# A transformer stack on one core: sparse attention worked in pairs of heads, products of ones placed in three waits of PE, and score maxima taken per query tile

## The chip, the core and the metric

The kernel is written in Bass, instruction by instruction, for one NeuronCore of a Trainium2 chip. The engines are PE (TensorE), DVE (VectorE), ACT (ScalarE), POOL (GpSimd) and SP, which issues most DMAs. Each runs its own list of instructions in order and waits on semaphores. The metric is the device time of one execution in microseconds (us), as the median of the runs shown.

## What is computed

Two blocks run one after the other on 256 tokens of 1,024 features, all in float32. The first has a state-space mixer with stick-breaking attention, cross attention to a memory, and a squared-ReLU feed-forward layer. The second has a gated convolution (its products are called pw1 and pw2 below), a convolutional feed-forward layer, the sparse attention that is changed here, and another feed-forward layer. The sparse attention of 16 heads of 64 features sums three branches, each with its own softmax and gate:

```python
return gt[..., 0:1] * o_c + gt[..., 1:2] * o_s + gt[..., 2:3] * o_w
```

`o_c` attends to 15 compressed keys. `o_s` (selected blocks) and `o_w` (window) see, at this length of 256 tokens, every key up to the query, with different keys and values: 4 groups of keys, each shared by 4 heads. So a branch of a head is a causal softmax over 256 keys: the first 128 queries see 128 keys, the second 128 queries see 256, together 384 columns of scores in 128 partitions.

## The kernel before

**Products of weights.** Weights stream from memory in chunks of 128x1024 numbers (`WR`). ACT rounds a chunk to the high part (`WH`, line 1254), DVE subtracts to get the low part (`WL`, line 1504), three chunks ahead of PE. `tile` multiplies a chunk with eight pieces (k = 0 to 7) of the activations, themselves in a high and a low part (`XH`, `XL` or `YH`, `YL`), three matmuls for each k (lines 876 to 878). Where the activations come just in time, the first tile waits for each k (`base=`), and with `norm=` it also sums the squares for the norm (`sum_square`, line 884, the product with `ONES`). `RS`, the factor of that norm, is only known when the tile has ended; DVE waits for it at the start of the program before it splits chunk 2.

**The first instructions.** PE waits for `ones_done`, then its first tile waits for chunk 0's low part and k = 0 of `XL`. DVE makes `XL` for k = 0 to 3, then `WL` of chunk 0 (`sp.to(1)`), then `XL` for the rest.

**Preparation of the sparse attention.** Twelve chunks of keys and queries pass through a per-head norm and a rotation. For the four chunks of keys, DVE adds the two terms of the rotation in two instructions of 64 partitions (line 638) into `KZ`, where the keys of the one head of a pair stand in partitions 0 to 63 and those of the other in 64 to 127, and the other half is zero.

**The attention.** One step is one head `hh`, both branches. Names: `big` holds the scores (2 of its 4 banks for a head), `mis` the turned weights, `acc` the outputs. The engines run these loops, each in the order written:

- PE: `scores` (two products and one of the mask for each branch, the queries as weights, all 128 rows), `turn` of the head before (6 transposes into `mis`), `outputs` of the head before that (6 products), and after each second head `pair`, which adds the compressed branch (line 493, 32 rows) and turns both heads' summed outputs (line 496).
- DVE: maxima of the scores (one instruction of 768 columns, line 781, which gives six numbers), a minimum of two of them (784), reciprocals of the sums (791), a copy of the second branch out of `mis` (795), the factors with the gates (798), the outputs times the factors (807), their sum (820), the low part `YL` (814).
- ACT: a copy of the first branch out of `mis` (586), four exponentials with their sums (593), the high part `YH` (605).
- POOL does nothing in it.

`scores` of a head waits for the exponentials two heads before (two buffers). The products of the output weights (`nsa_out`) follow.

## Time and profile before

| | |
|---|---|
| three runs | 1142.57, 1143.38, 1145.54 us; median 1143.38 |
| the profiled execution | 1141.42 us, span 1139.6 us |
| granted TensorE clock, mean | 0.988 of full |
| PE / DVE / ACT / POOL busy | 94% / 69% / 47% / 11% of the span |
| chain that ended last | PE 77%, DVE 13%, ACT 5%, issue 3%, POOL 1%, DMA 1% |

The span runs from the first to the last instruction of the profiled execution. A view over time gives for each row the start, the time to the end of the last one merged in it, engine, line and operation, the tile written and those read, the shape, and how many follow each other; in brackets the idle time before it and what ended it. The ends of matmuls are modelled and overlap the next, so the distance from one start to the next is what a matmul takes of PE. A float32 matmul stands as two instructions, one with the rounded types as one. A window gives its length, then for PE, PE's weight loads, DVE, ACT and POOL the busy time (and the instructions), the granted TensorE clock, the busy share of DMA, and GB/s. `64*128` stands for the rows and columns of the array that a matmul uses.

### The profile page before, as it was taken

To read this page: it belongs to the slowest core of one execution; us is meant where nothing else is said; L and a number is where in the kernel's file an instruction comes from. 1 tells how busy PE (TensorE), PEld (TensorE's weight loads), DVE (VectorE), ACT (ScalarE), POOL (GpSimd) and SP (SyncE) were. 2 spreads that over 40 slices of the span, in tenths; PEclk is the share of its full clock that TensorE was granted. 3 is DMA by queue.
4 is the path that set the end of the run, shared out by engine and by line. 5 is a ranking of instruction groups with operands and counts; after the bars stand their busy time and mean duration, and the time that the engine had idled before them with its cause. 6 is when DMAs were issued, how large, how long until landed. Compare 5 with 4: busy or idle time off the path is not lost.

```text
span 1139.6 us, 22909 instructions
## 1 busy us (share of the span) xinstructions
PE 1076.3 (94%) x8721; PEld 1023.1 (90%) x8721; DVE 788.4 (69%) x1314; ACT 534.6 (47%) x917; POOL 122.7 (11%) x140
## 2 busy tenths in 40 slices
PE   5999889799999989997999999997989999999998
PEld 4999679699999989877999999996878999999998
DVE  4876667655567767685776776759866667777676
ACT  5453555544443453217644444455435545444442
POOL 0060020011123300002001001040110000100100
PEclk9999999899999999999999999999999999999999
DMA  8563205255554634221565555663530025655551
GB/s 316 153 195 99 94 21 184 76 177 183 183 175 158 205 117 149 75 76 57 165 204 184 175 192 186 179 166 117 186 111 1 2 75 172 198 176 192 181 184 61
DMA packets 46438, 165.25 MB, mean 145 GB/s; under 512 B 5153, under 2 KB 6177, under 8 KB 46241
## 3 DMA queue, kind: packets, MB, share of 16 engines
q1 hardware_dynamic: 45216, 163.24, 45.1%
q10 hardware_dynamic: 1152, 1.05, 0.4%
q8 instruction: 49, 0.80, 0.3%
q14 instruction: 21, 0.16, 0.0%
HBM read 162.17 MB, written 1.05 MB: 143 GB/s over the span
## 4 chain that ended last, share of the span: by engine, by line
PE 77%; DVE 13%; ACT 5%; issue 3%; POOL 1%; DMA 1%; DVEq 0%; SPq 0%; ACTq 0%
PE acc L876 15%; PE acc L878 14%; PE acc L877 14%; PE big L876 6%; PE big L878 6%; PE big L877 6%; DVE WL L1504 4%; PE mis L884 2%; DVE CD L1871 2%; PE acc L480 2%; ACT WH L1254 2%; PE big L451 1%; PE acc L937 1%; PE acc L938 1%; PE acc L939 1%
## 5 line engine op out<-in xcount | busy, mean ns | idle before, releaser
L1504 DVE TENSOR_TENSOR WL<-WR,WH 128x1024 fp32r<-128x1024 f32 x302 | 378.8, 1269 | 148.4 <-ACT WH L1254 139.2
L876 PE MATMUL acc<-XH,WH 128*128 128x256 f32 x1392 | 404.8, 291 | 20.7 <-DVE WL L1504 13.2
L878 PE MATMUL acc<-XH,WL 128*128 128x256 f32 x1392 | 395.4, 284 | 0.0
L877 PE MATMUL acc<-XL,WH 128*128 128x256 f32 x1392 | 395.1, 284 | 0.0
L1254 ACT ACTIVATE WH<-WR 128x1024 fp32r<-128x1024 f32 x302 | 312.2, 1051 | 126.0 <-PE acc L878 82.7
L876 PEld LDWEIGHTS acc<-XH,WH 128*128 128x128 f32 x1392 | 268.2, 193 | 25.3 <-issue 17.8
L877 PEld LDWEIGHTS acc<-XL,WH 128*128 128x128 f32 x1392 | 267.8, 192 | 1.3
L878 PEld LDWEIGHTS acc<-XH,WL 128*128 128x128 f32 x1392 | 267.8, 192 | 0.0
L876 PE MATMUL big<-UH,WH 128*128 128x256 f32 x608 | 170.9, 281 | 0.9 <-POOL UL L1990 0.8
L877 PE MATMUL big<-UL,WH 128*128 128x256 f32 x608 | 169.6, 279 | 0.0
L878 PE MATMUL big<-UH,WL 128*128 128x256 f32 x608 | 169.6, 279 | 0.0
L1990 POOL TENSOR_TENSOR UL<-GU,UH 128x256 fp32r<-128x256 f32 x76 | 56.3, 741 | 679.0 <-ACT UH L1394 679.0
L876 PEld LDWEIGHTS big<-UH,WH 128*128 128x128 f32 x608 | 114.4, 188 | 1.9 <-POOL UL L1990 1.1
L878 PEld LDWEIGHTS big<-UH,WL 128*128 128x128 f32 x608 | 114.2, 188 | 0.0
L877 PEld LDWEIGHTS big<-UL,WH 128*128 128x128 f32 x608 | 114.1, 188 | 0.0
L1394 ACT ACTIVATE UH<-GU 128x256 fp32r<-128x256 f32 x76 | 31.8, 418 | 168.8 <-DVE GU L1782 95.6
L876 PE MATMUL acc<-YH,WH 128*128 128x256 f32 x256 | 75.9, 296 | 7.6 <-POOL YL L1986 6.5
L877 PE MATMUL acc<-YL,WH 128*128 128x256 f32 x256 | 73.2, 286 | 0.0
L878 PE MATMUL acc<-YH,WL 128*128 128x256 f32 x256 | 73.2, 286 | 0.0
L876 PEld LDWEIGHTS acc<-YH,WH 128*128 128x128 f32 x256 | 49.9, 195 | 10.7 <-issue 6.3
L877 PEld LDWEIGHTS acc<-YL,WH 128*128 128x128 f32 x256 | 50.1, 196 | 0.1
L878 PEld LDWEIGHTS acc<-YH,WL 128*128 128x128 f32 x256 | 49.9, 195 | 0.0
(296 smaller groups left out, 1294.7 us busy)
## 6 DMA issues: line engine op xcount, KB each, us to landing
WR<-weights SPq DMA_DIRECT2D x302, 512.0 KB, 3.6
X<-x_t SPq DMA_DIRECT2D x4, 256.0 KB, 6.2
MEM<-mem_t SPq DMA_DIRECT2D x1, 1024.0 KB, 9.7
result_t<-X SPq DMA_DIRECT2D x4, 256.0 KB, 2.2
CON<-constants SPq DMA_DIRECT2D x1, 896.0 KB, 11.8
CBUF<-KCV ACTq DMA_DIRECT2D x4, 128.0 KB, 5.4
CBUF<-KCV ACTq DMA_DIRECT2D x4, 127.5 KB, 6.5
SML<-small_weights SPq DMA_DIRECT2D x1, 480.0 KB, 14.2
```

What stands on the lines that cost most here:

```text
L451: pe.matmul(o[:, P:P + T], QP[:, j, P:T], k, start=False, stop=True, skip_group_check=True)
L480: ins = pe.matmul(acc[:, 0, (2 * br + tt) * P:(2 * br + tt) * P + P], PT[:, hh % 2, br, b * P:b * P + P], NV[:, m, 128 * g + 64 * br:128 * ...
L876: pe.matmul(out, wh, hi, start=start, stop=False, skip_group_check=True)
L877: pe.matmul(out, wh, lo, start=False, stop=False, skip_group_check=True)
L878: return pe.matmul(out, wl, hi, start=False, stop=stop, skip_group_check=True)
L884: ins = pe.matmul(mis[:, 0, 0:T], ONES[:, :], SQ[:, k], start=k == 0, stop=k == n - 1, skip_group_check=True)
L937: pe.matmul(o, xh, wh, start=kk == 0, stop=False, skip_group_check=True)
L1254: act.activation(WH[:, cs % SPL], WR[:, cs % RAW], ACT.Copy).then_inc(w_high, 1)
L1394: act.activation(UH[:, us % 2], GU[:, us % 2], ACT.Copy).then_inc(u_high, 1)
L1504: dve.tensor_tensor(WL[:, cs % SPL], WR[:, cs % RAW], WH[:, cs % SPL].bitcast(F32), ALU.subtract).then_inc(w_low, 1)
L1871: ins = dve.scalar_tensor_tensor(o, x, w, o, ALU.mult, ALU.add)
L1990: pool.tensor_tensor(UL[:, us % 2], GU[:, us % 2], UH[:, us % 2].bitcast(F32), ALU.subtract).then_inc(sem("u_low"), 1)
```

## The change

A step of the attention is now one branch of a pair of heads, still 16 steps. The scores of the two heads come from the two halves of the array's rows (64 features each, so `KR` needs no zeros), their outputs go through the two halves of its columns, and sum over branches in `acc` with the compressed branch, feature by feature, so the turn of the outputs is gone. The weights are normalised and gated before they are turned, by POOL, in three instructions. There are three buffers of weights instead of two, and `turn` and `outputs` run three and four steps behind `scores`. The second query tile's scores stand first in a bank, so that DVE takes the maxima in two instructions, one for each query tile, and the minimum is gone. `idle_passes` multiplies `ONES` with itself, 25 times at the start, 11 times before pw1 and 18 times before pw2; nothing reads the results. DVE makes `WL` of chunk 0 ahead of `XL`. PE waits for the seventh `YL` before `nsa_out`.

```diff
@@ -171,15 +171,15 @@
+                   ("QN", [P, 8, T], F32), ("QP", [P, 8, T], F32), ("KN", [P, 2, T], F32), ("KR", [P, 4, T], F32),
...
+        def PP(i):
+
+            flat = (CBUF.rearrange("p a g t -> p (a g t)")[:, 0:768], CBUF.rearrange("p a g t -> p (a g t)")[:, 768:1536],
+                    HS.rearrange("p a b t -> p (a b t)")[:, 1536:2304])[i % 3]
+            return flat.rearrange("p (e n) -> p e n", e=2)
+
+        PT = HS.rearrange("p a b t -> p (a b t)")[:, 0:1536].rearrange("p (s e n) -> p s e n", s=2, e=2)
@@ -439,63 +442,53 @@
+            pe.wait_ge(sem("kr_done"), 4)
...
+            def scores(i):
+                j, br = i // 2, i % 2
+                k = KR[:, 2 * br + j // 4, :]
+                if i >= 2:
+                    pe.wait_ge(sem("at_exp"), i - 1)
+                for q, o, n in ((slice(P, T), 0, T), (slice(0, P), T, P)):
+                    for e in range(2):
+                        h = slice(64 * e, 64 * e + 64)
+                        pe.matmul(big[:, 2 * br + e, o:o + n], QP[h, j, q], k[h, 0:n], start=o == 0, stop=True,
+                                  skip_group_check=True)
+                for e in range(2):
+                    ins = pe.matmul(big[:, 2 * br + e, P:P + T].rearrange("p (c n) -> p c n", c=2), IDR[:, :], NCR[:, :, :],
+                                    start=False, stop=True, skip_group_check=True)
                 ins.then_inc(sem("at_s"), 1)
 
+            def turn(i):
+                pe.wait_ge(sem("at_pn"), i + 1)
+                if i >= 1:
+                    pe.wait_ge(sem("at_pt"), i)
+                for e in range(2):
                     for b in range(3):
-                        ins = pe.transpose(mis[:, br, b * P:b * P + P], PP[:, hh % 2, br, b * P:b * P + P], con("ident"))
+                        c = (b + 1) % 3
+                        ins = pe.transpose(mis[:, e, c * P:c * P + P], PP(i)[:, e, b * P:b * P + P], con("ident"))
                 ins.then_inc(sem("at_t"), 1)
 
+            def outputs(i):
+                j, br = i // 2, i % 2
+                o = acc[:, j % 2, 0:T]
+                if br == 0:
+                    q = slice(32 * (j % 4), 32 * (j % 4) + 32)
+                    if j == 0:
+                        pe.wait_ge(sem("pct_done"), 1)
+                    if j >= 2:
+                        pe.wait_ge(yl_ready, Y_BASE["nsa"] + j - 1)
+                    pe.matmul(o, VB[q, j // 4, :], PCT[q, j // 4, :], start=True, stop=False, skip_group_check=True)
+                pe.wait_ge(sem("at_pt"), i + 1)
+                for m in range(2):
+                    for e in range(2):
+                        v = 128 * (2 * (j // 4) + e) + 64 * br
+                        ins = pe.matmul(o[64 * e:64 * e + 64, m * P:T], NV[:, m, v:v + 64],
+                                        PT[:, i % 2, e, m * T:m * P + T], start=False, stop=br == 1 and m == 1,
+                                        skip_group_check=True)
                 ins.then_inc(sem("at_o"), 1)
...
+            for i in range(STEPS + 4):
+                if i < STEPS:
                     scores(i)
-                if i == 1:
                     turn_compressed()
+                if 3 <= i <= STEPS + 2:
+                    turn(i - 3)
+                if i >= 4:
+                    outputs(i - 4)
@@ -578,37 +569,33 @@
+            for i in range(STEPS + 5):
+                if i < STEPS:
+                    act.wait_ge(sem("at_nm"), 2 * i + 2)
                     if i >= 3:
+                        act.wait_ge(sem("at_t"), i - 2)
+                    for e in range(2):
+                        for tt, (a, b) in ((1, (0, T)), (0, (T, P + T))):
+                            ins = act.activation(PP(i)[:, e, a:b], big[:, 2 * (i % 2) + e, a:b], ACT.Exp,
+                                                 bias=RM3[:, i % 3, e, 2 - 2 * tt:3 - 2 * tt],
+                                                 accum_out=RM[:, i % 3, 0, 2 * e + tt:2 * e + tt + 1])
+                            if (e, tt) != (1, 0):
                                 ch.add(ins)
                     ins.then_inc(sem("at_exp"), 1)
...
+                if i >= 6 and i % 2 == 0:
+                    j = (i - 6) // 2
+                    act.wait_ge(sem("at_o"), 2 * j + 2)
+                    act.activation(YH[:, j], acc[:, j % 2, 0:T], ACT.Copy).then_inc(yh_ready, 1)
@@ -632,10 +619,7 @@
-                    dve.wait_ge(sem("kz_zero"), 1)
-                    for e in range(2):
-                        h = slice(64 * e, 64 * e + 64)
-                        dve.tensor_tensor(KZ[h, e, n], T1[h, n % 2], T2[h, n % 2], ALU.add).then_inc(sem("kz_done"), 1)
+                    dve.tensor_tensor(KR[:, n], T1[:, n % 2], T2[:, n % 2], ALU.add).then_inc(sem("kr_done"), 1)
...
-                link(dve.memset(NV[:, :, 512:576], 0.0))
@@ -772,59 +755,47 @@
+            for i in range(STEPS + 5):
+                if 2 <= i <= STEPS + 1:
+                    r = RM[:, (i - 2) % 3]
+                    dve.wait_ge(sem("at_exp"), i - 1)
+                    dve.reciprocal(r[:, 1, :], r[:, 0, :]).then_inc(sem("at_inverse"), 1)
+                if i < STEPS:
                     dve.wait_ge(sem("at_s"), i + 1)
-                    m = RM3[:, i % 2]
-                    if i >= 2:
-                        dve.wait_ge(sem("at_exp"), i - 1)
-                    link(dve.tensor_reduce(m.rearrange("p b c -> p (b c)"),
-                                           big[:, 2 * (i % 2):2 * (i % 2) + 2, 0:384].rearrange("p b (c n) -> p b c n", c=3),
-                                           AX, ALU.max, negate=True))
-                    dve.tensor_tensor(m[:, :, 1:2], m[:, :, 1:2], m[:, :, 2:3], ALU.min).then_inc(sem("at_nm"), 1)
-                if i == 0:
+                    m = RM3[:, i % 3]
+                    for c, (a, b) in ((0, (0, T)), (2, (T, P + T))):
+                        dve.tensor_reduce(m[:, :, c], big[:, 2 * (i % 2):2 * (i % 2) + 2, a:b], AX, ALU.max,
+                                          negate=True).then_inc(sem("at_nm"), 1)
...
+                if 3 <= i <= STEPS + 2:
+                    dve.wait_ge(sem("at_t"), i - 2)
+                    if i >= 5:
+                        dve.wait_ge(sem("at_o"), i - 4)
+                    dve.tensor_copy(PT[:, (i - 3) % 2], mis[:, :, 0:384]).then_inc(sem("at_pt"), 1)
+                if i >= 6 and i % 2 == 0:
+                    j = (i - 6) // 2
                     dve.wait_ge(yh_ready, Y_BASE["nsa"] + j + 1)
+                    dve.tensor_tensor(YL[:, j], acc[:, j % 2, 0:T], YH[:, j].bitcast(F32), ALU.subtract).then_inc(yl_ready, 1)
 
         def pool_nsa(pool):
-            pool.memset(KZ[:, :, :, :], 0.0).then_inc(sem("kz_zero"), 1)
...
+            for i in range(STEPS):
+                j, br, g = i // 2, i % 2, RG[:, i % 3]
+                inverse = RM[:, i % 3, 1, :].rearrange("p (e t) -> p e t", e=2)
+                gate = GT.rearrange("p t (h x) -> p h t x", x=3)[:, 2 * j:2 * j + 2, :, 1 + br]
+                pool.wait_ge(sem("at_inverse"), i + 1)
+                if i == 0:
+                    pool.wait_ge(sem("gates"), 1)
+                for c, n, tt in ((0, 2, 1), (2, 1, 0)):
+                    pool.tensor_tensor(g[:, :, c:c + n], inverse[:, :, tt:tt + 1].broadcast_to([P, 2, n]),
+                                       gate[:, :, tt:tt + 1].broadcast_to([P, 2, n]), ALU.mult).then_inc(sem("at_rg"), 1)
+                pool.wait_ge(sem("at_rg"), 2 * i + 2)
+                x = PP(i).rearrange("p e (c n) -> p (e c) n", c=3)
+                pool.tensor_tensor(x, x, RG[:, i % 3].rearrange("p e c -> p (e c)").unsqueeze(2).broadcast_to([P, 6, P]),
+                                   ALU.mult).then_inc(sem("at_pn"), 1)
@@ -948,8 +919,14 @@
+            def idle_passes(t, n):
+
+                for _ in range(n):
+                    pe.matmul(acc[:, t % 2, 0:P], ONES[:, :], ONES[:, :], start=True, stop=True, skip_group_check=True)
+
             xl0 = (xl_ready, 8 * PREP["mix"])
             pe.wait_ge(sem("ones_done"), 3)
+            idle_passes(0, 25)
@@ -1167,6 +1144,8 @@
             sum_squares("final")
+            acc_ready(TILE["pw1"])
+            idle_passes(TILE["pw1"], 11)
@@ -1210,6 +1189,8 @@
             sum_squares("ln")
+            acc_ready(TILE["pw2"])
+            idle_passes(TILE["pw2"], 18)
@@ -1236,6 +1217,7 @@
             pe_nsa(pe, tile, token_major, three, rstd_columns, chunk_ready, acc_ready)
+            pe.wait_ge(yl_ready, Y_BASE["nsa"] + KD - 1)
             for j in range(KD):
@@ -1552,10 +1534,9 @@
             dve.wait_ge(sem("vec_loaded"), 16)
+            sp.to(1)
             for k in range(KD):
                 x_low("mix", k)
-                if k == 3:
-                    sp.to(1)
             sp.to(2)
```

The order of PE in the middle of the attention, for a pair of heads before (`KZ` with `QP` are scores, `NCR` the mask, `CON` with `CBUF` the transposes, `NV` with `HS` the outputs):

```order
L450 MATMUL big<-KZ,QP 128x128
L451 MATMUL big<-KZ,QP 128x256
L453 MATMUL big<-NCR,IDR 128x2x128
L450 MATMUL big<-KZ,QP 128x128
L451 MATMUL big<-KZ,QP 128x256
L453 MATMUL big<-NCR,IDR 128x2x128
L465 MATMUL mis<-CON,CBUF 128x128 x6
L480 MATMUL acc<-NV,HS 128x128 x6
L493 MATMUL acc<-H1T,VB 128x256
L496 MATMUL acc<-CON,GY 128x128 x2
```

and after, for two steps in the same place:

```order
L457 MATMUL big<-KR,QP 128x256 x2
L457 MATMUL big<-KR,QP 128x128 x2
L460 MATMUL big<-NCR,IDR 128x256 x2
L471 MATMUL mis<-CON,CBUF 128x128 x6
L488 MATMUL acc<-HS,NV 64x256 x2
L488 MATMUL acc<-HS,NV 64x128 x2
L457 MATMUL big<-KR,QP 128x256 x2
L457 MATMUL big<-KR,QP 128x128 x2
L460 MATMUL big<-NCR,IDR 128x256 x2
L471 MATMUL mis<-CON,HS 128x128 x6
L483 MATMUL acc<-H1T,VB 128x256
L488 MATMUL acc<-HS,NV 64x256 x2
```

The turn of the summed outputs (496) has left PE's list, and six products of outputs became four.

DVE at the start of the program, before (`XL` is the low part of the activations, `WL` that of a chunk):

```order
L1553 MEMSET KT 64x1024 x2
L1513 SCALAR_TENSOR_TENSOR XL<-X,VEC,XH 128x256 x4
L1504 TENSOR_TENSOR WL<-WR,WH 128x1024
L1513 SCALAR_TENSOR_TENSOR XL<-X,VEC,XH 128x256 x4
L1504 TENSOR_TENSOR WL<-WR,WH 128x1024 x3
L1521 TENSOR_TENSOR XP<-acc,RS 128x256
```

and after:

```order
L1535 MEMSET KT 64x1024 x2
L1486 TENSOR_TENSOR WL<-WR,WH 128x1024
L1495 SCALAR_TENSOR_TENSOR XL<-X,VEC,XH 128x256 x8
L1486 TENSOR_TENSOR WL<-WR,WH 128x1024 x3
L1503 TENSOR_TENSOR XP<-acc,RS 128x256
```

The chunk's low part moved ahead of the first four pieces of the activations.

## Rows read from the trace of the kernel before

**Rows 1.** windows, the attention: length, busy us of each engine, granted clock
```profile
850.10:921.69 71.59, 68.04 (x501) 61.76 (x500) 45.54 (x127) 38.39 (x152) 0.00 (x0) 1.00 0.02 8
```

**Rows 2.** PE over time, one head pair: start, us, operation, count
```profile
883.14 1.50 PE L480 MATMUL acc<-NV,HS 128*128 128x128 f32 x12
884.57 0.69 PE L493 MATMUL acc<-H1T,VB 32*128 32x256 f32 x2
885.19 0.71 PE L496 MATMUL acc<-CON,GY 128*128 128x128 f32 x4
885.74 0.39 PE L450 MATMUL big<-KZ,QP 128*128 128x128 f32 x2
...
887.29 0.81 PE L465 MATMUL mis<-CON,CBUF 128*128 128x128 f32 x6
887.94 1.28 PE L480 MATMUL acc<-NV,HS 128*128 128x128 f32 x10
```

**Rows 3.** groups, 850 to 922 us: count, busy us, mean ns, idle before
```profile
L593 ACT ACTIVATE CBUF<-big,RM 128x128 f32<-128x128 f32 x64 | 26.0, 419 | 5.6 <-DVE RM L784 5.0
...
L781 DVE TENSOR_REDUCE RM<-big 128x6 f32<-128x768 f32 x16 | 15.3, 957 | 9.2 <-PE big L453 9.0
...
L795 DVE COPY HS<-mis 128x384 f32<-128x384 f32 x16 | 8.5, 529 | 0.9 <-PE mis L465 0.9
```

**Rows 4.** PE over time, products on half the array columns
```profile
112.48 1.09 PE L1025 MATMUL big<-MM,MEM 128*64 128x128 f32 x16
```

**Rows 5.** POOL groups: count, busy, mean; then least, middle, most ns
```profile
L1976 POOL TENSOR_TENSOR DG<-CON,VEC 128x1152 f32<-128x1152 f32 x8 | 17.0, 2130 | 0.0
...
L1986 POOL TENSOR_TENSOR YL<-GY,YH x24: 724/735/1792, 58.6 to 527.2; 128x256 fp32r<-128x256 f32 x24
```

**Rows 6.** DVE over time, the start
```profile
9.16 1.11 DVE L1513 SCALAR_TENSOR_TENSOR XL<-X,VEC,XH 128x256 fp32r<-128x256 f32 x2 [5.94 <-ACT XH L1264]
...
11.60 1.22 DVE L1504 TENSOR_TENSOR WL<-WR,WH 128x1024 fp32r<-128x1024 f32 x1
...
22.66 2.42 DVE L1504 TENSOR_TENSOR WL<-WR,WH 128x1024 fp32r<-128x1024 f32 x2 [6.15 <-ACT RS L1275]
```

**Rows 7.** PE over time, the start, k by k
```profile
12.92 0.55 PE L876 MATMUL acc<-XH,WH 128*128 128x256 f32 x1 [12.92 <-DVE WL L1504]
...
14.19 0.78 PE L876 MATMUL acc<-XH,WH 128*128 128x256 f32 x1
...
15.68 0.78 PE L876 MATMUL acc<-XH,WH 128*128 128x256 f32 x1
...
18.11 0.47 PE L876 MATMUL acc<-XH,WH 128*128 128x256 f32 x1
...
18.89 0.47 PE L876 MATMUL acc<-XH,WH 128*128 128x256 f32 x1
```

**Rows 8.** PE over time, the first tile of pw1
```profile
419.77 0.36 PE L876 MATMUL acc<-XH,WH 128*128 128x256 f32 x1 [2.68 <-DVE XL L1513]
...
420.64 0.78 PE L876 MATMUL acc<-XH,WH 128*128 128x256 f32 x1
...
426.79 0.47 PE L876 MATMUL acc<-XH,WH 128*128 128x256 f32 x1
```

**Rows 9.** windows, 420.25 to 423.66 us, columns as in rows 1
```profile
420.25:423.66 3.41, 3.41 (x14) 2.96 (x13) 3.41 (x10) 3.41 (x10) 0.00 (x0) 0.50 0.00 0
```

**Rows 10.** DVE over time, end of the preparation before pw1
```profile
424.55 0.48 DVE L1513 SCALAR_TENSOR_TENSOR XL<-X,VEC,XH 128x256 fp32r<-128x256 f32 x1 [0.18 <-ACT XH L1264]
```

**Rows 11.** the first tile of pw2: PE, then POOL, over time
```profile
522.61 0.51 PE L876 MATMUL acc<-YH,WH 128*128 128x256 f32 x1 [4.62 <-POOL YL L1986]
...
521.74 6.22 POOL L1986 TENSOR_TENSOR YL<-GY,YH 128x256 fp32r<-128x256 f32 x8 [112.52 <-ACT YH L1449]
```

**Rows 12.** DVE groups, 765 to 792 us, before the attention
```profile
L638 DVE TENSOR_TENSOR KZ<-HS 64x256 f32<-64x256 f32 x8 | 3.4, 420 | 0.3
```

**Rows 13.** waits of PE, 765 to 792 us: us, times, longest us
```profile
PE mis L359 <- DVE KN L622: 3.9, 3, 1.3
```

130 lines of the change are left out of this document (11 added, 119 removed).

## The prediction

> **What bounds the kernel now.** The table of the profile comes first: PE is busy 94% of the span and 77% of the chain that ended last, so only what shortens PE's list or PE's waits counts. Then each place of the change is read by itself.
>
> In the attention, a window from the first score to the first product behind it is 71.6 us, and PE is busy 68.0 of them, DVE 45.5, ACT 38.4 [rows 1]. PE's list over time says what the 68 us are [rows 2], from start to start: 12 instructions of outputs take 1.43 us (884.57 - 883.14), the compressed branch 0.62, the turn of the outputs 0.55 (885.74 - 885.19), both branches' scores of a head 1.55 (887.29 - 885.74), six transposes 0.65. Two heads are 2 x (1.55 + 0.65 + 1.43) + 0.62 + 0.55 = 8.4 us, and eight such pairs 67.4 of the 71.6. So the attention is bound by PE; the rest, 4.2 us, are waits at its two ends. A float32 instruction of 128 columns takes 0.11 us here (1.43 less a pause of about 0.1, by 12), so one of 256 takes 0.22, and the mask, in the rounded type, 0.78 - 0.22 - 0.44 = 0.12.
>
> At the start PE does nothing for 12.9 us, and its last wait is for DVE's low part of chunk 0 [rows 7]. DVE began it at 11.60, behind four pieces of the activations, although it had been idle until 9.16 [rows 6]. Then PE ran slowly: a turn of k took 1.49 us (15.68 - 14.19) and later 0.78 (18.89 - 18.11), as at 1.2 and at 2.4 GHz [rows 7]. DVE split no further weights until the norm's factor came at 22.66 [rows 6]; DVE's list sets the pace of the tiles behind it.
>
> Before pw1 PE waits 2.68 us and then takes 7.02 us for seven turns of k [rows 8], with the granted clock at half in 3.41 us of them [rows 9]. Before pw2 it waits 4.62 us, and there the pieces come from POOL, eight in 6.22 us [rows 11]. In the preparation of the attention PE waits 3.9 us in three places for DVE [rows 13].
>
> **The attention, part by part.** A step after is one branch of two heads. *Scores*: per head one product of 256 columns and one of 128, each two instructions: 0.44 + 0.22 us if the two heads' halves of the array work side by side, twice that if not. Neither bound is shown for halves of rows by a row at full clock; the nearest is the product on half the columns, where 16 instructions of 128 columns take 1.09 us with the tail of the last, not 16 x 0.11 = 1.8 [rows 4]; with that tail, some 0.2 to 0.3, they run in pairs. I take side by side, 0.66, and keep 1.32 for the bad end. Two masks 0.24. *Transposes* 0.65 as before. *Outputs*: 256 and 128 columns on halves of the columns, 0.66. *Compressed branch*: 0.44 per two steps, 0.22. *Changes of the array's shape*: a step has four or five. The compressed branch shows their price: two instructions of 256 columns in 0.62 us instead of 0.44, and 0.1 ahead of it [rows 2], so 0.1 each, 0.5 a step. Sum: 0.66 + 0.24 + 0.65 + 0.66 + 0.22 + 0.5 = 2.95 us a step, where a head took 4.2.
>
> The Trainium skill (TensorEngine Tiling (Array Packing), Key Properties) speaks against the change here: a change of the tiling mode drains TensorE. The trace agrees, with about 0.1 us each. Without drains the step would be 2.45 us and the attention up to 8 us shorter; by the page they are paid, and it gives no time for them.
>
> The other engines in a step: *DVE* takes one reciprocal (0.17), two maxima of 512 and 256 columns (one of 768 takes 0.96 [rows 3]; two of them between 0.96 and 1.3, I take 1.1), a copy of 768 columns (two of the 0.53 for 384 are 1.06; with the fixed part once, 0.95 [rows 3]) and 0.2 of a low part: 2.4 us. *ACT* takes four exponentials of 0.42 [rows 3] and 0.2: 1.9. *POOL* is new. Its multiplication of 768 numbers is shown by no row. 1152 take 2.13 us, 256 take 0.73 at least [rows 5]; on the line between them 768 take 1.53, and the small ones 0.35 at most. Step: 1.53 + 2 x 0.35 + 0.1 = 2.3 us. The far ends are 3 x 0.73 = 2.2 for the large one (step 3.0), and the longest row, 1.79 for 256 [rows 5], below. So PE stays the bound with 2.95, and 16 steps are 47.2 us.
>
> To that come the ends. At the front the first weights come to PE only after scores 1.1, maxima (behind DVE's `NV`) about 1.8, exponentials 1.7, what DVE does for the compressed softmax about 2, POOL 2.3; PE has some five steps' worth of scores and a few transposes meanwhile, and stands about 3.5 us. At the back, after the last exponentials: reciprocal and POOL 2.5, transposes 0.8, copy 1.0, outputs 0.8, with about half of it covered by the steps before: 3 us. In between the loop over DVE and ACT (1.1 + 1.1 + 1.7 + latencies for two steps) is shorter than two PE steps, but the lists cross; I add 0.2 a step, 3.5. Sum 57.5 us against 71.6: **14.1 us less**. The stall that was at `pair` goes; next late is POOL's product, which `turn` waits for.
>
> **The start.** The piece for which DVE waited until 9.16 [rows 6] is made by ACT in 0.5 us right behind the high part of chunk 0, so DVE can begin that chunk at about 8.7 and end it at 9.9; the first piece of the activations takes 0.44, so PE starts at 10.4 instead of 12.92. The 25 products of ones take 0.22 us each at full clock and 0.43 at half: 10 in the first 4.3 us (PE was slow for as long, from 12.92 to about 17.2 [rows 7]), then 15 in 3.3, so from 1.1 to 8.8 us: over before 10.4. At full clock eight turns of k are 6.2 us, and the factor comes 1.0 behind them: 17.7 instead of 22.66. **4.9 us less**; 2.8 if the clock stays low (three turns at 1.49), which is the near bound. Nothing queued behind is nearer: the chunks 2 and 3 wait for that factor on DVE, and all tiles behind for DVE.
>
> **pw1.** 11 products of ones are 2.5 us, in a wait of 2.68. At 0.78 a turn, seven are 5.5 instead of 7.02: **1.5 us less**. The last piece is ready at 425.03 [rows 10], before 419.77 + 5.5 = 425.24, so it does not bind. If the ones ran over their gap, each would cost 0.22.
>
> **pw2.** 18 products are 4.0 us in a wait of 4.62; nothing. The gain is nothing too: the eighth piece comes at 527.96 (521.74 + 6.22) [rows 11], and POOL's 0.78 a piece was PE's pace at half clock anyway. At most 0.2.
>
> **The preparation.** DVE's two instructions of 0.42 become one of the same length [rows 12], four times 0.42 = **1.7 us less**, in a stretch where PE waits for DVE [rows 13]; between nothing and 2.1 (with the zeroing of `NV`). The wait for the seventh `YL` ahead of `nsa_out` costs nothing: it was made during the last step's outputs.
>
> Sum: 14.1 + 4.9 + 1.5 + 1.7 = 22.2 us. The profiled execution took 1141.4, so 1119.2 in its terms; the median of the runs shown lies 2.0 above it, so **1121 us**.
>
> **The rivals.**
>
> - *POOL sets the step.* If its product takes 2.2 us or more, a step costs POOL 3.0 and more and the attention 61 to 66 us: 1125 to 1130. For it: no row of this shape. Against: the row of 1152 numbers, taken beside DVE's work.
> - *The clock falls in or behind the attention*, or is not raised at the start: each fall costs some 1.5 us (pw1), the start 2.1: 1123 to 1127. For it: PE will stand a fifth of the attention. Against: the half clock at pw1 followed a wait of 2.68 us [rows 8]; the waits expected here are shorter.
> - *The halves do not run side by side.* Scores and outputs cost 1.3 us more, a step 4.3, the attention 72: 1135. Against: [rows 4].
> - *Slower than before: DVE holds POOL up.* Rows show POOL at 1.79 us where 0.73 is usual [rows 5], 2.4 times as long. With that factor on all three a step is 5.4 us, the attention about 92, the kernel 1155. It decides from a step of about 4.5 us on. Against: the long ones stand beside DVE's `WL`, with both inputs in SBUF; the maxima and copies here read PSUM. The skill (SBUF — State Buffer, Who interferes with whom) says the same: a DVE instruction with at most one SBUF input does not contend with GpSimd outside the two-port modes.
> - *The overlap is better than summed*, the ends shorter: 1113 to 1116.
>
> **How the numbers follow.** The forecast, 1116 to 1125, gets 0.53; POOL 0.18; the clock 0.12; better 0.07; no side by side 0.06; slower 0.04. The range must leave out no more than 0.2: from 1112 (all of the better case) to 1131 (all of POOL's and the clock's) it leaves out the last two cases and a little. A measurement tells 0.3% (3.4 us) from no change. Faster by more: all but the slower case and 0.02; within: 0.02; slower: 0.04.
>
> **What would show it.** In the profile after: the factor's first use by DVE at about 17.7 us; no stretch at half clock at pw1; the attention in 57 us, PE busy about 80% of it, the starts of two heads' score products in pairs; POOL's large product near 1.5 us. It is wrong if that product is over 2 us, if score products follow each other by 0.22 instead of in pairs, or if PE's first tile still runs at 1.49 a turn.

## The result, and the profile after

The changed kernel takes 1116.77 us (median of 4 runs, 1113.94 to 1118.27), the kernel before 1143.24 in the same session (4 runs, 1142.57 to 1145.54): ratio 0.9767, 95% interval 0.9755 to 0.978. The profiled execution took 1118.0 us with a span of 1116.1, so 23.5 us less span than before.

Where they came from is told by one instruction that stands in every stage: DVE's low part (`WL`) of the stage's first chunk of weights. Its start, in us, and how much earlier it is:

| first chunk of | before | after | earlier | forecast, from one row to the next |
|---|---|---|---|---|
| q | 34.30 | 29.46 | 4.84 | start 4.9 |
| pw1 | 405.32 | 400.88 | 4.44 | |
| pw2 | 485.33 | 479.27 | 6.06 | pw1 1.5 |
| ffn0 | 544.64 | 538.59 | 6.05 | pw2 nothing |
| nsa_q2 | 797.99 | 789.40 | 8.58 | preparation 1.7 |
| nsa_out | 839.67 | 832.11 | 7.56 | |
| ffn1 | 940.76 | 917.24 | 23.52 | attention 14.1 |

The attention, windows, against [rows 1] (first score to first product of `nsa_out`; second line: a stretch in it at half clock, a granted 0.50 or 1.2 GHz). Columns: window, length, busy us and instructions of PE, PE's weight loads, DVE, ACT, POOL, granted clock, DMA share, GB/s:

```profile
842.62:898.14 55.52, 51.64 (x405) 37.52 (x404) 37.90 (x79) 29.89 (x136) 28.86 (x48) 0.97 0.04 10
849.55:852.96 3.41, 3.41 (x18) 2.69 (x16) 1.18 (x4) 2.21 (x9) 3.25 (x5) 0.50 0.02 5
```

It takes 55.5 us where it took 71.6; PE is busy 93% of it. Two of its steps, PE over time, against [rows 2]:

```profile
871.71 0.92 PE L457 MATMUL big<-KR,QP 64*128 64x256 f32 x8
872.56 0.50 PE L460 MATMUL big<-NCR,IDR 128*128 128x256 f32 x2
872.90 0.82 PE L471 MATMUL mis<-CON,CBUF 128*128 128x128 f32 x6
873.65 0.69 PE L483 MATMUL acc<-H1T,VB 32*128 32x256 f32 x2
874.27 0.87 PE L488 MATMUL acc<-HS,NV 128*64 128x256 f32 x8
875.07 0.92 PE L457 MATMUL big<-KR,QP 64*128 64x256 f32 x8
...
877.82 0.92 PE L457 MATMUL big<-KR,QP 64*128 64x256 f32 x8
```

From score to score 3.36 us with the compressed branch and 2.75 without: 3.06 a step. By starts, the scores take 0.85 (872.56 - 871.71), the masks 0.34, the transposes 0.75, the compressed branch 0.62, the outputs 0.80. The work alone, by the prediction, is 0.66, 0.24, 0.65, 0.44 and 0.66; what is over is 0.19, 0.10, 0.10, 0.18 and 0.14: 0.71 with the compressed branch, 0.54 without, 0.62 a step, where the prediction has 0.5. The array's shape changes four times in the one step and three times in the other, not five: between the masks and the transposes it stays 128*128. By the starts of the single instructions (872.350, 872.558, 872.781, 872.898) a change adds about 0.09 us ahead of the first instruction of the new shape and up to 0.1 behind it, while the first transpose follows the last mask after 0.117 and pays nothing: 0.18 us a change.

The other engines in the attention, groups of instructions (count, busy us, mean ns, idle before them), against [rows 3]:

```profile
L775 DVE COPY HS<-mis 128x768 f32<-128x768 f32 x16 | 15.2, 949 | 3.1 <-PE mis L471 3.1
L767 DVE TENSOR_REDUCE RM<-big 128x2 f32<-128x512 f32 x16 | 10.9, 679 | 7.6 <-PE big L460 7.6
L767 DVE TENSOR_REDUCE RM<-big 128x2 f32<-128x256 f32 x16 | 6.6, 415 | 0.0
```
```profile
L797 POOL TENSOR_TENSOR CBUF<-CBUF,RG 128x768 f32<-128x768 f32 x11 | 16.2, 1469 | 0.9
...
L793 POOL TENSOR_TENSOR RG<-RM,GT 128x4 f32<-128x4 f32 x16 | 3.2, 203 | 36.9 <-DVE RM L762 36.9
L793 POOL TENSOR_TENSOR RG<-RM,GT 128x2 f32<-128x2 f32 x16 | 3.2, 197 | 0.0
```

POOL's large product takes 1.47 us and the small ones 0.2 each: 1.87 of POOL's time in a step. What PE waits for there (us in total, times, longest):

```profile
PE big L457 <- ACT CBUF L579: 1.6, 1, 1.6
PE mis L471 <- POOL CBUF L797: 1.2, 2, 0.8
PE acc L499 <- DVE GY L749: 1.0, 1, 1.0
```

The 1.6 and 1.0 are at the front, from 845.26 and 848.23 us on, and the stretch at half clock (849.55) follows them; POOL is waited for twice, at the back (890.95 and 895.26).

The start, PE and then DVE over time, against [rows 6, 7]:

```profile
1.06 8.41 PE L925 MATMUL acc<-ONES 128*128 128x128 f32 x50 [1.06 <-POOL EPS L1976]
10.23 0.35 PE L847 MATMUL acc<-XH,WH 128*128 128x256 f32 x1 [0.77 <-DVE XL L1495]
...
10.91 0.47 PE L847 MATMUL acc<-XH,WH 128*128 128x256 f32 x1
...
11.69 0.47 PE L847 MATMUL acc<-XH,WH 128*128 128x256 f32 x1
```
```profile
8.46 1.23 DVE L1486 TENSOR_TENSOR WL<-WR,WH 128x1024 fp32r<-128x1024 f32 x1 [5.26 <-ACT WH L1236]
9.61 1.78 DVE L1495 SCALAR_TENSOR_TENSOR XL<-X,VEC,XH 128x256 fp32r<-128x256 f32 x4
...
17.81 2.42 DVE L1486 TENSOR_TENSOR WL<-WR,WH 128x1024 fp32r<-128x1024 f32 x2 [1.61 <-ACT RS L1257]
```

A turn of k takes 0.78 us from the second on, and the factor is used at 17.81 instead of 22.66. At pw1, PE over time, against [rows 8]:

```profile
412.82 2.29 PE L925 MATMUL acc<-ONES 128*128 128x128 f32 x19
415.33 0.35 PE L847 MATMUL acc<-XH,WH 128*128 128x256 f32 x1 [0.23 <-DVE XL L1495]
...
416.04 0.44 PE L847 MATMUL acc<-XH,WH 128*128 128x256 f32 x1
...
416.83 0.43 PE L847 MATMUL acc<-XH,WH 128*128 128x256 f32 x1
```

The products of ones fill the wait, and the turns behind take 0.79.

The preparation, DVE over time, one chunk of keys, before and then after:

```profile
772.36 0.87 DVE L638 TENSOR_TENSOR KZ<-HS 64x256 f32<-64x256 f32 x2
773.26 0.48 DVE L622 SCALAR_TENSOR_TENSOR KN<-HS,VEC 128x256 f32<-128x256 f32 x1
```
```profile
766.06 0.42 DVE L622 TENSOR_TENSOR KR<-HS 128x256 f32<-128x256 f32 x1
766.40 0.48 DVE L609 SCALAR_TENSOR_TENSOR KN<-HS,VEC 128x256 f32<-128x256 f32 x1
```

From the start of the addition to the start of what follows it was 0.90 us and is 0.34: the one instruction saves 0.56, and not the 0.42 that one of them takes.

### The profile page after: what moved, and what is told of

Same layout as the page of the kernel before. It is cut to its first block, busy times and chain, and to the rows that moved or that the text cites. A ratio compares the mean times of both kernels' runs of the same rounds, so it can differ in the third digit from the quotient of the medians.

```text
span 1116.1 us, 22851 instructions
## 1 busy us (share of the span) xinstructions
PE 1071.4 (96%) x8733; PEld 1010.3 (91%) x8733; DVE 778.7 (70%) x1261; ACT 526.0 (47%) x901; POOL 149.8 (13%) x187
## 3 DMA queue, kind: packets, MB, share of 16 engines
q10 hardware_dynamic: 1152, 1.05, 0.4%
HBM read 162.17 MB, written 1.05 MB: 146 GB/s over the span
## 4 chain that ended last, share of the span: by engine, by line
PE 76%; DVE 13%; ACT 5%; issue 3%; POOL 1%; DMA 1%; DVEq 0%; SPq 0%; ACTq 0%
PE acc L847 15%; PE acc L849 15%; PE acc L848 15%; PE big L847 6%; PE big L849 6%; PE big L848 6%; DVE WL L1486 4%; PE mis L855 2%; DVE CD L1852 2%; ACT WH L1236 2%; PE big L457 1%; PE acc L908 1%; PE acc L909 1%; PE acc L910 1%; PE acc L488 1%
## 5 line engine op out<-in xcount | busy, mean ns | idle before, releaser
L1967 POOL TENSOR_TENSOR YL<-GY,YH 128x256 fp32r<-128x256 f32 x24 | 21.1, 899 | 243.9 <-ACT YH L1261 132.6
```

The costliest lines, as they stand in the source:

```text
L1967: pool.tensor_tensor(YL[:, k], GY[:, k], YH[:, k].bitcast(F32), ALU.subtract).then_inc(yl_ready, 1)
```

## The experiments

| kernel | us, median (range), runs | kernel before, same session | ratio, 95% interval |
|---|---|---|---|
| changed kernel again | 1118.09 (1112.10 to 1120.53), 6 | 1143.46 | 0.9778 [0.9755, 0.9801] |
| attention alone | 1124.97 (1122.58 to 1127.22), 4 | 1141.80 | 0.9854 [0.9829, 0.9878] |
| no ones at the start | 1119.95 (1114.26 to 1122.71), 5 | 1141.80 | 0.9798 [0.9768, 0.9828] |
| old order of DVE at the start | 1119.63 (1119.38 to 1123.58), 5 | 1141.80 | 0.9808 [0.9787, 0.9829] |
| no ones at pw1, pw2 | 1118.04 (1115.55 to 1122.74), 5 | 1141.80 | 0.9804 [0.9778, 0.9830] |
| scores head by head | 1116.86 (1113.99 to 1118.07), 4 | 1142.11 | 0.9780 [0.9765, 0.9796] |
| POOL's product twice | 1125.95 (1125.48 to 1128.03), 4 | 1142.11 | 0.9860 [0.9843, 0.9878] |
| ones at the attention's front | 1113.46 (1112.64 to 1117.05), 5 | 1142.11 | 0.9747 [0.9734, 0.9761] |
| ones in nine waits | 1115.56 (1110.16 to 1116.71), 5 | 1142.11 | 0.9765 [0.9748, 0.9782] |
| maxima in one instruction | 1126.73 (1122.93 to 1127.30), 4 | 1143.46 | 0.9860 [0.9846, 0.9875] |
| both heads on one half of the rows | 1133.88 (1130.48 to 1135.76), 4 | 1143.46 | 0.9927 [0.9908, 0.9945] |
| ones in more waits, later turn | 1110.57 (1110.45 to 1113.68), 5 | 1143.46 | 0.9729 [0.9714, 0.9744] |

One kernel's executions lie up to 8 us apart, more than most parts of the change are worth. So each part is read from the profiled execution, as a difference between two `WL` starts (as above), and the medians only bear it out. All kernels below are edits of the changed one.

**The changed kernel again.**

> The changed kernel as it is, beside the others of this call on the same chip, so that they have a measure nearer than the kernel before. 1116.8 us, with executions from 1112 to 1120 by how many stretches at half clock there are and how late the activations arrive at the start.

1118.09 us; profiled, its `WL` starts lie within 0.15 us of the first execution's, with the clock down at the same six places.

**The attention alone.**

```diff
-            idle_passes(0, 25)
-            acc_ready(TILE["pw1"])
-            idle_passes(TILE["pw1"], 11)
-            acc_ready(TILE["pw2"])
-            idle_passes(TILE["pw2"], 18)
-            sp.to(1)
             for k in range(KD):
                 x_low("mix", k)
+                if k == 3:
+                    sp.to(1)
```

> The changed attention and preparation stay; the products of ones are gone at all three places and DVE's order at the start is the old one. If the parts simply add, as the prediction has them, it loses the start (4.9 us) and pw1 (1.5) against the changed kernel: 1116.8 + 6.4 = 1123.2 us, and 20.0 less than the kernel before, all of it at the attention (16) and its preparation (1.5 to 2.5). Rival: the start's gain is not kept to the end, since the stages between are paced by other things (0.4 us of it had gone by pw1): then it takes 1121 or less. The half clock should stand at pw1 again and the tiles of the first stage run 1.49 us a turn of k.

1124.97 us in the median, 1122.58 in the profiled execution. The `WL` starts are 5.30 us late at q (0.46 of it is a start later than before's own), 5.08 at pw1, 6.70 at pw2 and 6.70 at ffn0. So the start is kept almost whole, pw1 gives 1.62, and the parts add. The rival falls. By nsa_out the difference is 4.11, since its clock was down for 3.41 us in the preparation where the changed kernel's was for 10.24, and by ffn1 4.56, since it was down for 3.41 us more in the attention.

**The two halves of the start.** First the products of ones gone (`-            idle_passes(0, 25)`):

> Only the 25 products of ones ahead of the first tile are gone; DVE's new order stays. If they raise the clock and PE then takes 1.49 us a turn for some three turns, PE starts at 10.2 as before and the factor comes 2.1 us later: 1118.9 us. Rival: DVE, which makes each piece of the activations in 0.42 us, or the arriving activations set the pace of the first tile; then the products of ones bring nothing and it stays at 1116.8.

Then DVE's old order (the last part of the diff above), with the products of ones kept:

> Only DVE's order at the start is the old one (chunks 0 and 1 split behind four pieces of the activations); the products of ones stay. PE's first product then starts at 12.9 instead of 10.2 us, 3.4 us behind the last product of ones. If the clock stays up over that wait: 2.7 us later, 1119.5 us. Rival: the clock falls in the wait, and both halves of the start's gain are lost: 4.9 us, 1121.7.

Without the ones, PE over time has its turns of k at 1.49 us until 14.36, and DVE uses the factor at 20.15:

```profile
11.37 0.78 PE L847 MATMUL acc<-XH,WH 128*128 128x256 f32 x1
...
12.86 0.78 PE L847 MATMUL acc<-XH,WH 128*128 128x256 f32 x1
```
```profile
20.15 2.42 DVE L1485 TENSOR_TENSOR WL<-WR,WH 128x1024 fp32r<-128x1024 f32 x2 [4.09 <-ACT RS L1256]
```

That is 2.34 us late at q, near the expected 2.1; the rival, that they bring nothing, falls.

With the old order, PE and then windows: the clock had risen at 5.29 us, and was back at half from the first product on, as the rival had it; the `WL` at q is 3.52 us late, not the rival's 4.9.

```profile
1.05 7.86 PE L925 MATMUL acc<-ONES 128*128 128x128 f32 x50 [1.05 <-POOL EPS L1977]
12.12 0.58 PE L847 MATMUL acc<-XH,WH 128*128 128x256 f32 x1 [3.21 <-DVE WL L1486]
```
```profile
12.11:15.53 3.42, 3.41 (x12) 3.05 (x13) 2.64 (x5) 3.33 (x7) 0.00 (x0) 0.50 1.01 416
```

The factor is used at 22.66 us with neither edit, 20.15 with the order alone, 21.33 with the ones alone, 17.81 with both. But chunk 0 also arrives at another time in each execution: ACT begins to round it at 7.60, 7.16, 6.85 and 7.30 us. From there to the factor's use it is 15.06, 12.99, 14.48 and 10.51 us. So the order alone is worth 2.1, the ones alone 0.6, both 4.55, and 0.3 of the 4.85 is an earlier arrival. One edit keeps the other's gain, since a wait of 3.21 us behind the ones undoes them. A late arrival does the same with both edits: in the profiled execution of *POOL's product twice*, below, ACT begins at 8.33, PE waits 2.35 us behind the ones, the clock falls at 12.13 and the factor is used at 20.45. (The old order's `WL` at xq is 5.7 us late, 2.2 of it from a longer and a further stretch at half clock in that execution.)

**No ones at pw1 and pw2.**

```diff
-            acc_ready(TILE["pw1"])
-            idle_passes(TILE["pw1"], 11)
-            acc_ready(TILE["pw2"])
-            idle_passes(TILE["pw2"], 18)
```

> The products of ones are gone ahead of pw1 and pw2 only. By the prediction pw1 loses 1.5 us and pw2 nothing: 1118.3 us, with 3.41 us at half clock at pw1 and seven turns of k in about 7.0 us instead of 5.5. Rival: pw1's loss is given back behind it, because the following stage waits for DVE and not for PE: 1116.8.

Between the `WL` starts of pw1 and pw2 it loses 1.61 us, from pw2 to ffn0 0.79. Windows of the two stretches at half clock:

```profile
415.26:418.67 3.41, 3.41 (x13) 3.05 (x13) 3.41 (x10) 3.41 (x9) 0.00 (x0) 0.50 0.00 0
517.66:524.48 6.82, 6.75 (x28) 6.10 (x27) 0.48 (x1) 4.96 (x12) 4.58 (x7) 0.50 0.00 0
```

In the kernel before the stretch at pw2 lasted 3.41 us, and lay in the time in which POOL sets the pace anyway; here it lasted 6.82 and cost 0.8. So the 18 products are worth nothing or 0.8, by the execution. Yet this profiled execution was 2.5 us shorter than the changed kernel's: its start was 0.9 earlier, its clock was down for 6.8 us in the preparation instead of 10.2 (2.7 us gained by nsa_out), and it stayed up in the attention, which took 54.24 us instead of 55.52. That is the price of that fall: 1.28 us.

**Scores head by head.**

```diff
-                for q, o, n in ((slice(P, T), 0, T), (slice(0, P), T, P)):
-                    for e in range(2):
+                for e in range(2):
+                    for q, o, n in ((slice(P, T), 0, T), (slice(0, P), T, P)):
```

> The score products are issued head by head, both products of one head and then both of the other, so that only where the heads meet can two row halves of the array work side by side. The result is the same. If the halves work side by side as the prediction took it (0.66 us for eight instructions and not 1.32), most of that is lost: about 0.5 us in each of 16 steps, 8 us, 1125 us, and the starts of the scores follow each other by 0.22 and 0.11 us instead of in pairs. Rival: the pairs in the trace are only starts, and the work takes as long either way: 1117.

1116.86 us, a step without the compressed branch 2.75, as in the changed kernel (scores start at 877.16 and 879.91).

Neither theory holds as written. The single instructions start in pairs still, the second head's 13 ns behind the first's (877.161 and 877.174) instead of 6, though four instructions of the first are issued ahead of it. The edit does not take the pairing away, so this run could not price it.

**Both heads on one half of the rows.**

```diff
-                        h = slice(64 * e, 64 * e + 64)
+                        h = slice(0, 64)
                         pe.matmul(big[:, 2 * br + e, o:o + n], QP[h, j, q], k[h, 0:n], start=o == 0, stop=True,
```

> Both heads' scores are made from the rows 0 to 63 (the first head's queries and keys), so the second head's scores are the first's; the number and size of the instructions stay. The order of issue did not keep the halves apart in the run before; here both chains need the same half of the rows. If the halves working side by side is what makes eight instructions take 0.66 us and the drains, they now take 1.32, and a step 3.06 + 0.66 = 3.7: 10.5 us more, 1127 us. Rival: PE hides part of it where it waits anyway (it is busy 98 of 100 in the middle of the attention, so little): 1125. If time stays at 1117, the pairing is no gain of the change.

1133.88 us. PE over time, one step, then windows, a stretch at its front:

```profile
873.13 1.57 PE L457 MATMUL big<-KR,QP 64*128 64x256 f32 x8
874.63 0.50 PE L460 MATMUL big<-NCR,IDR 128*128 128x256 f32 x2
```
```profile
845.24:865.72 20.48, 19.71 (x71) 14.56 (x71) 7.91 (x17) 6.96 (x32) 7.49 (x14) 0.50 0.00 1
```

The scores take 1.50 us from start to start instead of 0.85: 0.65 a step, 10.4 in 16 steps, as expected. The attention grew by 17.0 (72.54 us); the rest, 6.6, goes with the clock, at half for 20.48 us where the changed kernel had 3.41 (about 1.3 for each 3.41 us), though PE is busy in 19.71 of them. Why it stayed down is not shown.

**POOL's product twice.**

```diff
-                pool.tensor_tensor(x, x, r, ALU.mult).then_inc(sem("at_pn"), 1)
+                pool.tensor_tensor(x, x, r, ALU.mult).then_inc(sem("at_rg"), 1)
+                pool.wait_ge(sem("at_rg"), 3 * i + 3)
+                pool.tensor_tensor(x, x, r, ALU.mult).then_inc(sem("at_pn"), 1)
```

> POOL multiplies the weights of each step twice, so that they are left scaled by the square of the factor; all else is the same. POOL then has 2 x 1.47 + 2 x 0.2 + 0.1 = 3.4 us of work in a step, where PE has 3.06. If the step is set by the engine with the most work, as the prediction has it, the attention grows by 16 x 0.35 = 6 us and by one product at its front and back, 3 us: 1126 us. Rival: the loop through PE, DVE, ACT and POOL, with its waits, is already nearly as long as the room that three buffers give; then each added us is paid in full in each step, 16 x 1.47 = 23 us: 1140.

1125.95 us. POOL over time, the first product of one step and of the one two steps on, and PE's waits:

```profile
868.79 1.47 POOL L798 TENSOR_TENSOR CBUF<-CBUF,RG 128x768 f32<-128x768 f32 x1
...
875.88 1.47 POOL L798 TENSOR_TENSOR HS<-HS,RG 128x768 f32<-128x768 f32 x1
```
```profile
PE mis L471 <- POOL CBUF L800: 8.4, 7, 2.0
PE mis L471 <- POOL HS L800: 2.5, 3, 1.1
```

A step is 7.09 / 2 = 3.55 us, POOL's own work in it 3.4, and in every second step it waits 0.23 for DVE's reciprocal: POOL sets the step. The window of the attention:

```profile
841.01:906.47 65.46, 51.84 (x405) 36.50 (x404) 39.10 (x79) 29.88 (x136) 52.19 (x64) 1.00 0.03 9
```

It takes 65.46 us, at full clock throughout although PE waits 12 times in it, 13.5 us together, 11.2 more than the 54.24 of the changed kernel at full clock, where 23 would be paid if each added us counted. So POOL's 1.9 us a step have about 1.2 us of room under PE's 3.06. The rival "POOL sets the step" had its mechanism right and its price (61 to 66), and not its condition.

**Maxima in one instruction.**

```diff
-                    for c, (a, b) in ((0, (0, T)), (2, (T, P + T))):
-                        dve.tensor_reduce(m[:, :, c], big[:, 2 * (i % 2):2 * (i % 2) + 2, a:b], AX, ALU.max,
-                                          negate=True).then_inc(sem("at_nm"), 1)
+                    link(dve.tensor_reduce(m[:, :, :], big[:, 2 * (i % 2):2 * (i % 2) + 2, 0:384].rearrange(
+                        "p e (c n) -> p e c n", c=3), AX, ALU.max, negate=True))
+                    dve.tensor_tensor(m[:, :, 0:1], m[:, :, 0:1], m[:, :, 1:2], ALU.min).then_inc(sem("at_nm"), 2)
```

> The maxima of a step are taken as in the kernel before: one DVE instruction over 768 columns in six blocks of 128, and a small minimum behind it, that waits for it. DVE has about 2.4 us of work in a step of 3.06, so 0.2 us more of it hides: 1116.8 us. Rival: the loop from scores to exponentials to POOL is what sets the step at its ends, where POOL's product was late for the transposes; then the exponentials come 0.2 us later (or earlier, if one instruction is faster than two) and a step of the front and back pays it: up to 0.5 us either way.

1126.73 us; the attention takes 65.19 instead of 55.52. Both theories miss by far. The small minimum, two numbers a row: count, then least, middle and most ns; who waited for it (us, times):

```profile
L768 DVE TENSOR_TENSOR RM<-RM x16: 163/863/1050, 840.4 to 891.4; 128x2 f32<-128x2 f32 x16
...
  ACT CBUF L579: 19.4, 9
```

And over time, with POOL's product beside it:

```profile
883.42 1.47 POOL L797 TENSOR_TENSOR HS<-HS,RG 128x768 f32<-128x768 f32 x1
...
883.86 1.05 DVE L768 TENSOR_TENSOR RM<-RM 128x2 f32<-128x2 f32 x1
...
884.83 0.95 DVE L775 COPY HS<-mis 128x768 f32<-128x768 f32 x1
```

The minimum takes 0.163 us in the three steps where POOL stands still as it starts. In the other 13 POOL's product is running, and it ends 0.016 to 0.021 us behind it (884.911 and 884.891 here), whether that is 0.2 or 1.05 us after its start. POOL's product takes 1.47 with or without it. The minimum is DVE's one instruction in a step with both inputs in SBUF; the maxima, the copy and `YL` read PSUM and keep their times. The kernel before had it already, where POOL's product of 1152 numbers meets DVE's `WL`, with two inputs in SBUF as well:

```profile
332.40 2.13 POOL L1976 TENSOR_TENSOR DG<-CON,VEC 128x1152 f32<-128x1152 f32 x1
```
```profile
L1504 DVE TENSOR_TENSOR WL<-WR,WH x302: 1206/1219/3007, 11.6 to 1126.1; 128x1024 fp32r<-128x1024 f32 x151
```

The eight `WL` that start 0.2 us behind such a product take 3.00 us instead of 1.22 and end 1.08 behind it; the four products of POOL of 1.6 to 1.8 us, [rows 5], start behind a `WL` and end 0.60 behind it. So whichever starts second is held until the first has ended. That is what the Trainium skill says (SBUF — State Buffer, Who interferes with whom): a DVE instruction with two SBUF inputs contends with a GpSimd instruction that reads SBUF. The trace agrees, with up to 0.89 us for each. Behind the minimum everything is late: ACT's exponentials, and DVE's copy, for which PE waits 5.7 us in four places (longest 2.5). The clock is at half for 13.65 us in the attention instead of 3.41. PE stands idle for 8.6 us in it instead of 3.9, and three more stretches of 3.41 us at 1.28 each would be 3.8, so by this estimate 4.7 of the 9.7 us are waits and most of the rest is the clock; they were not measured apart.

**Ones at the attention's front.**

```diff
             for i in range(STEPS + 4):
+                if i == 2:
+                    pe.wait_ge(acc_free, TILE["nsa_out"])
+                    idle_passes(0, 7)
                 if i < STEPS:
                     scores(i)
                 if i == 2:
+                    idle_passes(0, 4)
                     turn_compressed()
```

> Adds 7 and 4 products of ones in PE's two waits at the front of the attention (1.6 and 1.0 us). If those waits bring the half clock of 3.41 us that follows them, it goes, and the attention is 1.3 us shorter, as in the profiled execution where it did not fall: 1115.5 us. Rival: the fall has its cause further back (the small products and waits of the preparation), and moves or stays: 1116.8.

1113.46 us. The window of the attention:

```profile
842.95:897.20 54.25, 52.78 (x427) 38.87 (x426) 37.86 (x79) 29.88 (x136) 28.86 (x48) 1.00 0.04 11
```

54.25 us, as in the execution whose clock stayed up by itself, so the expected 1.3 is there. That the products of ones brought it, this one execution does not show: with both waits left open the front had no fall in two of ten profiled executions (*no ones at pw1, pw2* and *POOL's product twice*). With the waits filled it had none in three of three, this one and the two kernels that follow. Elsewhere the clock fell otherwise than in the changed kernel: not at 88 us, for 6.83 us at 119.46, and for 3.41 at 157.00. The medians' intervals overlap with the changed kernel's.

**Ones in nine waits.** The edit above, and products of ones in seven more waits of PE, of which this is the first:

```diff
             for i in range(SB_HEADS + 2):
+                if i == 2:
+                    for _ in range(14):
+                        pe.matmul(mis[:, 1, 256:384], ONES[:, :], ONES[:, :], start=True, stop=True, skip_group_check=True)
```

> Adds products of ones in nine waits of PE: 14 before the third score product of the mixer (a wait of 3.7 us), 12 and 8 in the cross attention (2.8 and 2.1), 7 before the second compressed product (1.7), 9 before the hidden layer is turned (2.3), 4 and 4 at the last normed tiles (1.0 each), and 7 and 4 at the front of the attention. Stretches at half clock were 3.4 us (mixer), 6.8 (cross attention), 6.8 and 3.4 (preparation) and 3.4 (attention), with 1.0 to 1.6 us lost in each 3.4 us. If the waits bring them, all but the one at 88 us go: 7 to 9 us less than the changed kernel, 1109 us. Rival: small or narrow products bring them as well as waits, so that half of them stay: 1113; and where products of ones run over their wait they cost 0.2 each.

In the profiled execution, 1110.16 us, the clock falls once, at 774.99 for 3.41 us; the `WL` starts gain 1.4 us on the changed kernel at mem_v, 4.0 at ff and 7.9 at ffn1. The first of these is the fall at 88 us, which vanished though nothing was added there. The median, 1115.56, is no better than that of the kernel above: its other executions have a mean clock of 0.992 to 0.997 where the profiled one has 0.998. At this point the rival stands.

**Ones in more waits, and a later turn.** On top of the nine waits:

```diff
-            idle_passes(0, 25)
+            idle_passes(0, 28)
...
+                if n in (4, 5):
+                    acc_ready(normed_tile(n) + 1)
+                    idle_passes(normed_tile(n) + 1, 3)
                 if n >= 2:
                     rotate(n - 2)
...
-                if i == 2:
-                    idle_passes(0, 4)
+                if i == 3:
                     turn_compressed()
+                    idle_passes(0, 3)
```

> The kernel with products of ones in nine waits, and three edits more: 28 products of ones instead of 25 at the start (0.8 us of wait were left behind them, and in one execution 2.3 with a fall of the clock in it), 3 ahead of each of two rotations in the preparation (waits of 0.76 us, ahead of the one fall of the clock that was left, which cost 1.0), and the turn of the compressed weights one step later, where PE need not wait for DVE's compressed softmax. If waits bring the falls: 1.0 for the fall, 0.5 for the turn, and fewer slow starts: 1108.5 in its best execution and 1113 in the median. Rival: the falls that are left come at other places in other executions, so that the median stays with that of nine waits, 1115.6.

1110.57 us, 7.5 less than the changed kernel on the same chip, and the intervals of the two ratios do not meet; three of five executions have a mean clock of 1.000 and the others 0.997 and 0.998. Window from the clock's first rise to its fall at the end:

```profile
7.26:1109.76 1102.50, 1072.30 (x8860) 1013.85 (x8859) 777.48 (x1258) 524.83 (x900) 149.40 (x180) 1.00 0.47 149
```

With the waits filled, then, hardly a fall is left in five executions, where no execution of the changed kernel has a mean clock above 0.994; most of the falls hang on the waits, and filling them goes with most of the 7.5 us. That each wait brings its fall is not so: twelve waits passed without one in *POOL's product twice*. Nor is a wait always there. Ahead of the fall at 88.38 us in the changed kernel PE has none over 0.1 us from 76 us on, but 32 narrow products, 3.5 us of them:

```profile
83.52 3.63 PE L945 MATMUL mis<-SML,G 128*128 128x8 f32 x32
```

So for this fall the rival, narrow products, is left standing; it is gone in the last three kernels without an edit there, and why is open. The later turn was a miss: the attention takes 54.67 us, 0.43 more than with nine waits.

## Why the prediction was right, step by step

The forecast was 1121 us, the kernel takes 1116.8, within the range. What bounds each stage and what the edits free was right. Sizes were off in both directions and in part cancelled: the ends of the attention and the preparation gave more, the steps and a fall of the clock that was not expected took some back. That the sum came so near is in this part luck.

- *What bounds the kernel*: PE, right. Without waits and falls the attention follows PE's list (38.9 us busy of 39.7 between 852.96 and 892.64).
- *The start, 4.9*: 4.84, of which 0.3 is that chunk 0 arrived earlier than in the execution of before from which the sum was made. At the same arrival it is 4.55; that 4.84 meets 4.9 is luck. The two edits' shares, which the prediction did not part, are not independent.
- *pw1, 1.5*: 1.62 by both kernels. *pw2, nothing*: nothing here, 0.8 in another execution.
- *The preparation, 1.7*: 2.53 by nsa_q2, above the upper bound of 2.1, then 1.00 given back by nsa_out, where the clock was down 6.83 us (805.18) instead of 3.41. The 1.7 was mis-sized: the prediction counted the 0.42 us of one instruction, but four times the 0.56 from start to start are 2.3, and without the zeroing of `NV` DVE is 0.25 earlier; together 2.5.
- *PE's step, 2.95*: 3.06. The pairs (0.66) stand, shown by one half of the rows with 0.65 a step more. The outputs on the two halves of the columns take 0.80 for eight instructions, the changes included, and start in pairs; no run took them apart. The changes of shape were counted as four or five at 0.1 each, and are three or four at 0.18: 0.62 a step instead of 0.5; that is the step's error. [rows 2] had the price: around the compressed branch a pause of 0.1, 0.62 instead of 0.44, and 0.55 instead of 0.44 for the four instructions behind it are 0.4 for two changes, of which the prediction left out the last part. The Trainium skill (TensorEngine Tiling (Array Packing), Key Properties) has both, tiles that operate independently and a drain at a change of mode; the trace agrees with both (0.85 us on two halves of the rows against 1.50 on one; 0.18 a change).
- *POOL, 2.3*: 1.87. The line through two rows gave 1.53 for the product that takes 1.47; the small ones were bounded by 0.35 and take 0.2.
- *The ends and the slack*: this is the term that was mis-sized. The prediction's terms, front 3.5, back 3 and 3.5 for 0.2 a step, make 10.0 and with 47.2 the attention 57.2; its 57.5 has 0.3 too much. At full clock the attention is 54.24, and 16 x 3.06 = 48.9 leaves 5.3 instead of the 10.3. PE waits at the front for 2.6 us, and at the back for 1.2; a slack in every step is not there, for PE has no other wait over 0.25 us. So 57.5 + 1.7 (steps) - 5.0 (ends) + 1.3 (clock) = 55.5 us, 2.0 less than forecast. The ends are what the rival of the better overlap had, with a chance of 0.07.
- *The clock's rival*: its argument fell. It was held against it that the half clock at pw1 followed a wait of 2.68 us and the waits here would be shorter; they were 1.6 and 1.0, and the clock fell. It cost 1.28 and was hidden by the ends. The trace of before had the like, which the prediction did not weigh: in the preparation the clock fell at 833.26 us with waits of only 1.00 and 1.02 us (ended at 830.49 and 833.17) ahead of it.
- *The halves do not run side by side*: its time does not follow from its terms. 16 steps of 1.3 us more are 21, so the attention would be 78 and the kernel 1142, not 72 and 1135. Either time lies outside the range.
- *Slower, DVE holds POOL up*: POOL's product keeps its 1.47 us. The danger was the other way round: had the change kept the small minimum, POOL would have held DVE up, and 9.7 us of the attention's gain would have been lost. The trace of before showed it in eight `WL` of 3.00 us, and the prediction read only the other direction from it. The prediction costed the two maxima at 1.1 against 0.96 us and saw only that as their price; what they save was not in it.
- The rest between 22.2 and 23.5: attention +1.9, preparation -0.2, pw1 +0.1, and 0.4 lost between the start and pw1.

## What to carry to other kernels

Before work is moved to POOL, look at DVE's instructions in the same loop for those with two inputs in SBUF, however small: each may wait for the whole of POOL's instruction. Two instructions from PSUM were cheaper than one and a minimum of two numbers. Where PE stands for a us or more, products of ones in the wait are worth what the clock costs where it falls behind it, 1.3 us (in the attention) to 1.6 (at pw1) for 3.41 us at half clock here; but a wait left between them and the work undoes them, so the order that shortens the wait comes first. And where executions of one kernel differ by more than the parts of a change, compare the start of one instruction that stands in every stage, and list the falls of the clock beside it.

## What was not expected of the hardware

- DVE's minimum of two numbers in each row ended 0.016 to 0.021 us behind POOL's product in 13 of 13 cases where that was running, up to 1.05 us long instead of 0.163.
- The order in which products for the two halves of the rows are issued did not matter: the second half's began 13 ns behind the first's with four of the first half's issued between.
- The same wait is followed by a fall of the clock in one execution and not in another: the waits of 1.6 and 1.0 us at the attention's front by 3.41 us at half clock, or by none (no ones at pw1 and pw2, and POOL's product twice, whose ten further waits of up to 2.0 us no fall followed either). In the attention alone and head by head the clock fell at the end of the first of the two, for 6.83 us. Head by head has the changed kernel's waits in the preparation too, but no fall there, where the changed kernel was at half clock for 10.24 us, and is 4.1 us shorter by it. The fall at 88 us comes in most kernels and is gone in three, in stretches where the code is the same. What decides it was not found out.
- The clock stayed at half for 20.48 us with PE busy in 19.71 of them, in the kernel whose scores used one half of the rows.
